# Separate instruction lists for three engines in the mixing stage of a two-layer hybrid block

## What is computed

```python
for l in range(2):
    proj = rms_norm(x, norm_mix_g[l]) @ w_in[l]          # x is 256 x 1024
    pa, pb, pc, pg = split(proj)
    oa = rwkv7_time_mix(pa, ...)          # 8 heads of 64; group norm over the heads at its end
    ob = stick_breaking_attention(pb)     # 8 heads of 64
    oc = differential_attention(pc, ...)  # 4 heads, two softmax maps each
    ga, gb, gc = split(sigmoid(pg), 3)
    merged = ga * (oa @ w_branch_a[l]) + gb * (ob @ w_branch_b[l]) + gc * (oc @ w_branch_c[l])
    x = x + merged @ w_out[l]
    x = x + conv_ffn(rms_norm(x, norm_ffn_g[l]), ffn_w_up[l], ffn_conv_w[l], ffn_conv_b[l], ffn_w_down[l])
return rms_norm(x, norm_final_g)
```

## Time and profile before

| | us |
|---|---|
| median of 3 runs | 1132.0 |
| the runs | 1129.6, 1132.0, 1133.97 |
| the profiled execution, its own time | 1134.54 |
| its span | 1132.7 |
| mean granted TensorE clock | 0.989 of full speed |

### The profile page before, as it was taken

How to read it: one execution, slowest core, us unless ns; L and a number is a source line. 1 busy time by engine, 2 the same in 40 slices (tenths; PEclk the granted TensorE clock), 3 DMA queues, 4 the chain that set the end, 5 groups by cost and what they waited for, 6 DMA issues and landing times.

```text
span 1132.7 us, 26059 instructions
## 1 busy us (share of the span) xinstructions
PE 1088.8 (96%) x10078; PEld 1030.0 (91%) x10078; DVE 829.4 (73%) x1393; ACT 596.0 (53%) x883; POOL 10.5 (1%) x24
## 2 busy tenths in 40 slices
...
GB/s 279 135 165 76 112 76 94 66 149 138 143 129 187 140 197 185 186 184 169 190 128 142 157 58 110 61 85 109 136 166 131 131 186 168 186 187 183 169 186 112
DMA packets 46272, 164.00 MB, mean 145 GB/s; under 512 B 5904, under 2 KB 6080, under 8 KB 46192
## 3 DMA queue, kind: packets, MB, share of 16 engines
...
q10 hardware_dynamic: 720, 1.14, 0.3%
...
HBM read 161.24 MB, written 1.05 MB: 143 GB/s over the span
## 4 chain that ended last, share of the span: by engine, by line
PE 73%; DVE 14%; ACT 7%; issue 5%; DMA 1%; ACTq 0%; DVEq 0%; SPq 0%
PE psum L457 73%; DVE sb_lo L1196 3%; ACT sb_rw L862 3%; ACT sb_inv L862 2%; ACT sb_hi L862 1%; DVE sb_rw L1274 1%; DVE sb_inv L1408 1%; DVE sb_yf L1422 1%; DVE sb_small L1477 1%; DMA sb_x<-x_t 1%; DVE sb_rw L1259 0%; ACT L862 0%; DVE sb_rw L1333 0%; DVE sb_inv L1400 0%; DVE sb_ol L1215 0%
## 5 line engine op out<-in xcount | busy, mean ns | idle before, releaser
L457 PE MATMUL psum<-sb_hh,sb_hi 128*128 128x256 f32 x1568 | 458.3, 292 | 11.1 <-DVE sb_rw L1259 4.2
L457 PE MATMUL psum<-sb_hl,sb_hi 128*128 128x256 f32 x1568 | 446.5, 285 | 0.0
L457 PE MATMUL psum<-sb_hh,sb_lo 128*128 128x256 f32 x1568 | 446.1, 285 | 0.0
L862 ACT ACTIVATE sb_hi<-sb_raw 128x1024 fp32r<-128x1024 f32 (+1 forms) x300 | 312.9, 1049 | 237.3 <-PE psum L457 233.1
L1196 DVE TENSOR_TENSOR sb_lo<-sb_raw,sb_hi 128x1024 fp32r<-128x1024 f32 x298 | 363.5, 1221 | 100.3 <-ACT sb_hi L862 98.4
L457 PEld LDWEIGHTS psum<-sb_hh,sb_hi 128*128 128x128 f32 x1568 | 303.4, 193 | 22.3 <-issue 16.3
L457 PEld LDWEIGHTS psum<-sb_hl,sb_hi 128*128 128x128 f32 x1568 | 303.7, 194 | 2.2 <-issue 2.2
L457 PEld LDWEIGHTS psum<-sb_hh,sb_lo 128*128 128x128 f32 x1568 | 303.6, 194 | 0.0
L457 PE MATMUL psum<-sb_oh,sb_hi 128*128 128x256 f32 x672 | 193.1, 287 | 7.9 <-DVE sb_ol L1525 4.7
L457 PE MATMUL psum<-sb_oh,sb_lo 128*128 128x256 f32 x672 | 190.8, 284 | 0.0
L457 PE MATMUL psum<-sb_ol,sb_hi 128*128 128x256 f32 x672 | 190.8, 284 | 0.0
...
## 6 DMA issues: line engine op xcount, KB each, us to landing
...
```

The source lines that it names most:

```text
L457: return pe.matmul(out, lhsT, rhs, start=start, stop=stop, skip_group_check=True)
L862: return act.activation(out, in_, func, scale=scale, bias=bias, **kw)
```

## The change

It replaces `mixing_steps` by a fixed row of the small steps (`WORK`) and three strings, from which `placed` builds an own list for each engine: "+k" takes the next k small steps, "D5-7" and "E5" put slabs and their emptying between them. It also:

- puts "gn1" ahead of "bz, 0" in the row, and "gn3", "gn4" later among the scores;
- places the gates in units 1, 2, 5, 0, 3, 4 (`GATE_UNIT`), so that G0 to G11 need no unit that the group norm reads; a sigmoid of two units becomes two instructions;
- transposes the two maps of a head of the second attention in one step "ct" (three transposes, then two copies on ACT), four steps a layer and not eight;
- lets "upg" wait for the first four sigmoids of "up" alone; moves the wait for the inversion from "rhs0" to "u0";
- exchanges two branch slabs, ("BR", 1, 2) with ("BR", 2, 0);
- gives the output slabs banks 5, 6, 7, 3, drops the wait after slab 81, and multiplies output slabs 0 and 1 in turns: input tiles 0 to 5 of both, then 6 and 7 of both.

```diff
-         + [("BR", *bc) for bc in ((1, 0), (1, 1), (2, 0), (1, 2), (2, 1), (1, 3), (2, 2), (2, 3))]
+         + [("BR", *bc) for bc in ((1, 0), (1, 1), (1, 2), (2, 0), (1, 3), (2, 1), (2, 2), (2, 3))]
...
-BANK = [0, 1, 2, 5] + [(m - 4) % 3 for m in range(4, len(OUTS))]
+BANK = [0, 1, 2, 5] + [(m - 4) % 3 for m in range(4, len(OUTS) - KT)] + [5, 6, 7, 3] * 2
...
+STEPS = placed(
+    "+ D0-2 +2 D3-5 +2 D6 + D7-8 + D9-10 + D11 +3 D12-15 + D16 +2 D17-18 + D19 +2 D20 +2 D21 +2 D22 +21 D23 +5 "
...
+ACT_STEPS = placed(
+    "+ D0-1 + D2-3 E0 + D4 E1 + E2-3 D5 E4 + E5-6 D6-7 + D8-9 + E7-8 D10 E9 + E10 D11 E11 D12 + D13 + E12-13 + "
...
+DVE_STEPS = placed(
+    "+ D0-1 E0 + D2 E1 D3 + E2 D4 + E3 + E4-5 D5 E6 + D6 + D7 E7 D8-9 E8-9 D10 E10 + E11 + D11-12 E12 D13 E13 + "
...
-        GATE = unit(0, 6).rearrange("p (b c t) -> p b c t", b=3, t=T)
+        GATE_UNIT = (1, 2, 5, 0, 3, 4)
...
+            def two_of_output(l, n):
...
+                for part in (range(0, 6), range(6, KT)):
+                    for i in range(2):
+                        s, out = (n + i) % RING, bank[BANK[OUT_OF[n + i][0]]][:, 0:T]
+                        for k in part:
+                            if i == 0 and k % 2 == 0:
+                                pe.wait_ge(merged_l, l * (KT // 2) + k // 2 + 1)
...
-                    pe.wait_ge(act_["up"], n_of("up", l, 1))
+                    pe.wait_ge(act_mid["up"], n_of("up", l, 1))
...
-                    pe.wait_ge(dve_["dxy"], n_of("dxy", l, ORD[("dxy", c | 1, LEVELS[-1])] + 1))
...
+                    if kind == "u0":
+                        pe.wait_ge(dve_["dxy"], n_of("dxy", l, ORD[("dxy", c | 1, LEVELS[-1])] + 1))
...
+                    for n, (tt, b) in enumerate(((0, 0), (1, 0), (1, 1))):
+                        last = pe.transpose(bank[7][:, n * P:(n + 1) * P], PC[:, tt, 0, b * P:(b + 1) * P],
+                                            cst("ident"))
...
-                pe.wait_ge(*n_out(l, len(OUTS) - 1))
...
-                    g = unit(2 * c, 2) if c < 2 else unit(2 + c)
-                    do(g, g, ACT.Sigmoid).then_inc(gates_ready, 1)
+                    for i in ((1, 2), (5, 0), (3,), (4,))[c]:
+                        ins = do(unit(i), unit(i), ACT.Sigmoid)
+                    ins.then_inc(gates_ready, 1)
```

More of the change, by code:

```diff
@@ L163 @@
-STEPS = mixing_steps()
-DVE_STEPS = list(STEPS)
-for _i in range(len(STEPS) - 1):
-    if STEPS[_i][0] == "D" and STEPS[_i + 1][0] == "E":
-        DVE_STEPS[_i], DVE_STEPS[_i + 1] = STEPS[_i + 1], STEPS[_i]
+WORK = [
+    ("xs", 0), ("norm", 0), ("lam",), ("lora",), ("up",), ("upg",), ("kkq",), ("kk",), ("kkn",), ("prepa",),
+    ("prepb",), ("rk",), ("bon",), ("natv",), ("natk",), ("mat", 0, "ab"), ("mat", 0, "abt"), ("mat", 0, "akb"),
+    ("mat", 1, "ab"), ("mat", 1, "abt"), ("mat", 1, "akb"), ("m1", 0, 2), ("m1", 1, 2), ("dxy", 0, 2), ("dxy", 1,
[4 rows of a table added]
+    ("mat", 2, "ab"), ("mat", 2, "abt"), ("mat", 2, "akb"), ("mat", 3, "ab"), ("mat", 3, "abt"), ("mat", 3, "akb"),
[5 rows of a table added]
+    1), ("gn3",), ("rope", 0), ("bav", 0), ("btri", 1), ("bz", 2), ("rope", 1), ("gn4",), ("bav", 1), ("bz", 3),
+    ("btri", 2), ("bav", 2), ("btri", 3), ("bav", 3), ("cs", 0, 0), ("gsig", 0), ("cs", 0, 1), ("gsig", 1), ("ct",
+    0), ("cs", 1, 0), ("cs", 1, 1), ("cav", 0), ("ct", 1), ("cs", 2, 0), ("cs", 2, 1), ("cav", 1), ("ct", 2), ("cs",
+    3, 0), ("cs", 3, 1), ("cav", 2), ("ct", 3), ("cav", 3), ("crms",), ("gsig", 2), ("gsig", 3), ("xs", 1)]
@@ L169, with placed @@
+def placed(text):
+    out, rest = [], list(WORK)
+    for word in text.split():
+        kind, _, span = word[0], word[0], word[1:]
+        if kind == "+":
+            for _ in range(int(span or 1)):
+                out.append(rest.pop(0))
+        else:
+            first, _, last = span.partition("-")
+            out += [(kind, n) for n in range(int(first), int(last or first) + 1)]
+    return out + rest
+STEPS = placed(
[4 rows of a table added]
+ACT_STEPS = placed(
[7 rows of a table added]
+DVE_STEPS = placed(
[7 rows of a table added]
 TIMES = {}
@@ L370, in hybrid_blocks @@
         dve_mid = {k: sem("dve_mid_" + k) for k in ("lam", "prepb", "bon", "cs", "crms")}
[L371 removed]
+        act_mid = {k: sem("act_mid_" + k) for k in ("up", "crms")}
         x_mm, x_done = sem("x_mm"), sem("x_done")
```

118 lines of the change are left out of this document (30 added, 88 removed), and 24 rows, old and new, of tables (ACT_STEPS, DVE_STEPS, STEPS, WORK).

## The result

The changed kernel takes **1101.1 us** (median of 4 runs, 1100.96 to 1101.27) where the kernel before takes 1133.0 in the runs beside it (4 runs, 1129.6 to 1136.4): a ratio of 0.972, interval 0.969 to 0.975, so 32 us less. The forecast was 1103. The profiled execution took 1101.0, its span is 1099.2.

The account below looks back on a forecast made before the run. PE was taken as the bound, busy 1088.8 of 1132.7 us. 23.5 + 1.4 + 4.8 + 1.6 + 4.2 - 5.6 = 29.9 off 1134.5 gives 1104.6; 1102 at the median's level, plus 1 for handovers: 1103, range 1091 to 1119.

Parts of the forecast that it names:

- Waits that go: PE's 18 waits from the mixing's order, 20.6 us idle plus 0.16 each, were to go: 23.5 us.
- Output slabs: Slab 74's wait for merged tiles shrinks by about 0.7 us a layer through multiplying output slabs 0 and 1 interleaved: 1.4.
- Longer groups: Slab runs in the mixing fall from 50 to 38 a layer; 0.2 us gained per join: 4.8, between 2.4 and 6.5.
- Inversion's last level: PE's wait before "dxy" of level 64 goes, with a slab between the two "m1": 0.8 us a layer, 1.6.
- Clock: Three falls of PE's clock behind gaps that go, 1.4 us each: 4.2; the fall at 176.50 stays.
- two signs named as wrong: PE waiting for `sb_lo` inside the mixing, or low-clock windows in new places, would show the prediction wrong.
- Added costs: New waits before "cav, 0" (1.7), at "rhs1" (0.4), in the second inversion (0.4), at slab 69 (0.3): 5.6 us in all.
- Sum: Whole kernel: 29.9 us off the profiled 1134.5 gives 1104.6; on the median's level 1102; plus 1 for handovers, 1103.
- Everything fits: Rival, chance 0.2: "cav, 0" does not wait, small waits and the fall at 176.50 go, joins give 6.5: 1093 us.
- DVE paces the mixing: Rival, chance 0.2: lo parts come too late at tight places, waits only move, some 15 us gained: 1117.
- The switches of ACT's tables: Rival, chance 0.02: four loads before "cav, 0" each hold ACT twice 1.28 us, PE waits 10 us more: 1113.
- The slower side: Rival, chance 0.03: ACT's splits ahead of short work stall PE, 2.9 us each; seven such places a layer give 1143.

Follow-up runs that it names:

- the next one: Changed kernel with sigmoids joined, slab 60's split earlier, output pair four and four, branch norm in halves: 1092.9 us; with slab 60's DVE step later as well: 1095.0.
- three of the experiments: Against the changed kernel: ACT's and DVE's lists by the old rule, 1135.1 us; slabs at old places with own lists, 1140.9; the same placed by name, 1137.9.

## Why the prediction was right, point by point

**Waits that go (23.5).** Right, and slightly low. All 18 went. By step times the places where they stood (slabs 6, 9, 15, 38 and 81, "bz, 1", "o, 3", "cav, 1", "cav, 3", "ct, 3") are 12.6 us a layer shorter, clock falls left out: 25.3. The walk through the lists was the right tool: it said that nothing new would stand at "gn2", slab 41 and slab 9, and nothing did. What the prediction did not say is how little of this any single edit does. It gave the wait before "upg" to the four sigmoids and to "lora" one emptying earlier; the sigmoids are 0.32 of 1.19.

**Output slabs (1.4).** Size right (0.8 a layer against 0.7), reason wrong. The sum gave it to the interleave of slabs 74 and 75, and undoing that costs 0.07. The lists give the 0.8. The prediction took it that DVE's order there is unchanged, and the sum is near by luck.

**Longer groups (4.8).** The step that failed, although its number came out. The 0.2 us that a slab gains by a join are real (0.17 measured), but the small product in front of another small product loses 0.15: eight of the twelve joins undone cost 0.01 each. The prediction said that this was "not shown by a row"; the rows of "bon" and slab 17 in the earlier trace rows's kind of window would have shown it. What is left for the term: the mixing is 2.2 us a layer shorter once the other terms are taken off. It lies in many steps that stood 0.1 to 0.3 above their pace before (slab 13 3.15 to 2.88, between two slabs in both kernels; slab 59 3.18 to 2.88, alone before and now between two slabs). How much of that is lists and how much places, the runs do not separate. That 4.4 comes near 4.8 is luck.

**Inversion's last level (1.6).** Right: from "m1, 0, 64" to slab 24, 6.17 us where it had been 6.64, twice a layer, so 1.9.

**Clock (4.2).** Three falls were to go, and went. The one at 176.50, which the prediction kept ("follows the inversion, was not there in layer 1, and stays"), went too (slab 33 took 4.47 and takes 3.06), and so did one in the very first slab, at 9.6 to 13.0, which took 6.24 and takes 6.04. One came new at the end of layer 0. Windows of the changed kernel at 176.50, at the place where layer 0 ends, and at the end:

```profile
176.50:181.00 4.50, 4.50 (x25) 3.89 (x24) 2.73 (x3) 1.50 (x3) 0.00 (x0) 1.00 0.57 161
...
544.50:549.00 4.50, 3.46 (x21) 3.49 (x22) 4.35 (x8) 3.72 (x7) 0.00 (x0) 0.76 0.60 190
...
1084.50:1089.00 4.50, 4.32 (x25) 4.35 (x26) 3.25 (x6) 3.10 (x4) 0.00 (x0) 0.69 0.03 7
```

Of the two signs named as wrong, PE waits for `sb_lo` only once, 1.1 us ahead of slab 1 of layer 0, while the first slabs come in, and one low-clock window is in a new place. Net about 4.9: 5.7 for the four, 1.2 back for the new one, 0.4 for a shorter last one.

**Added costs (-5.6).** The wait ahead of "cav, 0" is 1.70 in both layers where 1.7 was worked out, from ACT's and PE's work counted from one common start. "s1, 2" to "o, 2" takes 0.55 a layer more (forecast 0.4). The emptyings in the second inversion cost nothing (0.4): the levels stay at 3.07. The wait of slab 69 for "crms" is there, but it is not new. The kernel before has it too, one slab earlier, at its own branch slab ("BR", 2, 0):

```profile
PE psum L457 <- DVE sb_ol L1500: 0.9, 2, 0.5
```

From "crms" through the second slab behind it the step times are 8.20 in both layers before and 8.27 and 8.09 now, so this part costs nothing (0.3). Together 2.2 to 2.4 a layer by step times, 4.6, where 5.6 was forecast. What the prediction says of the drain behind a table load came out right, but not from the row that it names: the 0.0 in the earlier trace rows is the idle time ahead of the loads. The time behind them is in the experiment with two more loads, 0.01 us.

**Sum.** By term, profile against profile: 25.3 + 1.6 + 4.4 (the 2.2 of both layers) + 1.9 + 4.9 - 4.6 = 33.5, and 33.6 was measured (1134.5 to 1101.0). That it closes shows little, since the 4.4 is what the other terms leave. Forecast 29.9, nearly 4 short: 1.8 of it in the waits, 1.0 in the added costs, 0.7 in the clock, 0.3 in the inversion. The forecast of the time was nearer than that, and that is luck, because a second step failed the other way: 2.5 us were taken off to come from the profiled execution to the median. What set the profiled one above the median was most likely the clock (last section), and its falls had been counted as gains already. The changed kernel's profiled execution lies on its median.

**The rivals.** Of them "Everything fits" is the nearest: the fall at 176.50 went and no handover showed, but "cav, 0" waits, so 1101 and not 1093. "DVE paces the mixing" did not come about in the changed kernel, yet it shows in the next one: the wait that only moves from "ct, 2" to "ct, 3". The switches of ACT's tables cost their own 1.28 us. The rule of the Trainium skill ("ScalarE: Activation LUTs", Table sets: the hidden batching unit) is to batch calls by set. The trace agrees in part: joined, the sigmoids take PE's wait of 1.7 us away, and 1.3 of it come back ahead of slab 60. The slower side, lists and places that do not meet, is what three of the experiments are: 1135 to 1141. The prediction gave it 0.03 for the lists as they are, and described its mechanism as a split in front of short work; the case found is an emptying in front of short work (slab 38 ahead of "gn1"), 3.9 us each.
